# The first expert block of a decoder step: rows by one-hot products, its down product ahead of the second block

## The reference, cut to what matters

```python
def hierarchical_moe(h, w_rg, b_rg, w_re, b_re, w_gate, w_up, w_down):
    t = h.reshape(B * S, D)                       # D = 1024, h = RMSNorm(x) * (1 + scale2) + shift2
    g_logits = (t @ w_rg) + b_rg                  # 4 groups
    g_probs, g_sel = softmax(g_logits), argmax(g_logits)
    e_logits = ((t @ w_re) + b_re).reshape(-1, 4, 8)   # 8 experts in each group, the chosen group's are used
    top_p, top_i = top_k(softmax(e_logits), 2)
    gate = one_hot(g_sel * 8 + top_i) * (g_w * top_p / sum(top_p))
    for g in range(4):
        hid = silu(t @ w_gate) * (t @ w_up)       # per expert 1024 -> 256
        out += (hid * gate) @ w_down              # per expert 256 -> 1024
# x += gate2 * moe(h)
```

## Time and profile before

| | us |
|---|---|
| median of 3 runs (lowest, highest) | 767.51 (767.08, 767.58) |
| the profiled execution, its whole time | 769.74 |
| its span in the profile | 768.0 |
| TensorE busy in the span | 740.7 (96%) |
| VectorE, ScalarE, GpSimd busy | 409.4, 205.9, 166.9 |
| TensorE's share of the chain that ended last | 78% |
| transfers' share of that chain | 7% |

### The profile page before, as it was taken

One profiled execution on the slowest core, in us unless ns is written; L12 is line 12 of the kernel. 1 busy time (PEld: TensorE's weight loads), 2 busy tenths in 40 slices (PEclk: granted clock), 3 DMA queues, 4 the chain that ended last, 5 costly groups with the idle time before them and its releaser, 6 DMA issues.

```text
span 768.0 us, 11157 instructions
## 1 busy us (share of the span) xinstructions
PE 740.7 (96%) x4239; PEld 464.9 (61%) x4239; DVE 409.4 (53%) x955; ACT 205.9 (27%) x419; POOL 166.9 (22%) x188
## 2 busy tenths in 40 slices
PE   7999999999999999997999999999999999999986
PEld 6545465688756657885888544657555555555541
DVE  4124399999999998610254234874432232222235
ACT  4012253306567676002000011222111111111112
POOL 2031021140000000074400002543333333333210
PEclk9999999999999999998999999999999999999999
DMA  8972064123256265453232843359999999999988
GB/s 332 429 252 96 0 218 159 34 91 116 108 212 229 110 242 203 142 181 105 94 101 101 321 190 131 133 183 357 422 422 427 425 424 423 425 425 424 423 336 329
DMA packets 29673, 187.72 MB, mean 244 GB/s; under 512 B 7296, under 2 KB 8384, under 8 KB 18224
## 3 DMA queue, kind: packets, MB, share of 16 engines
q1 hardware_dynamic: 19168, 164.98, 53.8%
q0 software_dynamic: 9536, 19.72, 7.8%
q10 hardware_dynamic: 912, 2.26, 0.8%
HBM read 180.89 MB, written 16.13 MB: 257 GB/s over the span
## 4 chain that ended last, share of the span: by engine, by line
PE 78%; DVE 8%; DMA 7%; issue 3%; ACT 3%; SPq 1%; POOL 0%; DVEq 0%; ACTq 0%; POOLq 0%
PE psum L842 23%; PE psum L1334 13%; PE psum L809 12%; PE psum L1348 7%; DMA ring<-in_experts 5%; PE psum L754 3%; PE psum L1233 3%; PE psum L675 2%; PE psum L1327 2%; DMA ring<-expert_rows 2%; DVE arena L2339 1%; DVE arena L2337 1%; DVE arena L2338 1%; PE psum L658 1%; PE psum L940 1%
## 5 line engine op out<-in xcount | busy, mean ns | idle before, releaser
L842 PE MATMUL psum<-hT,ring 128*128 128x260 f32 x640 | 147.1, 389 | 5.9 <-issue 3.8
L842 PEld LDWEIGHTS psum<-hT,ring 128*128 128x128 f32 x640 | 122.2, 193 | 30.3 <-issue 8.8
L1818 ACT ACTIVATE arena<-psum 128x512 f32<-128x512 f32 (+10 forms) x127 | 68.2, 571 | 228.6 <-PE psum L658 50.9
L809 PE MATMUL psum<-ring,hT 128*128 128x512 f32 (+1 forms) x256 | 93.1, 517 | 0.0
L809 PEld LDWEIGHTS psum<-ring,hT 128*128 128x128 f32 x256 | 47.4, 190 | 41.8 <-issue 32.6
L1334 PE MATMUL psum<-ring,arena 128*64 128x256 f32 x608 | 69.0, 379 | 2.2 <-DMA ring<-in_experts 1.4
L1348 PE MATMUL psum<-arena 128*64 128x512 f32 x280 | 67.8, 605 | 1.4 <-issue 1.4
L1750 POOL DMA_INDIRECT expert_rows<-arena,router x34 | 34.5, 1014 | 139.7 <-DVE arena L2850 123.3
L1334 PEld LDWEIGHTS psum<-ring,arena 128*64 128x64 f32 x608 | 43.8, 137 | 31.3 <-issue 10.1
L2843 DVE COPY arena<-psum 128x128 f32<-128x128 f32 x35 | 10.2, 292 | 95.6 <-PE psum L1341 80.8
L842 PE MATMUL psum<-arena,ring 128*128 128x260 f32 x256 | 58.9, 386 | 0.0
(11 more groups left out here) (402 smaller groups left out, 960.5 us busy)
## 6 DMA issues: line engine op xcount, KB each, us to landing
ring<-in_stream SPq DMA_DIRECT2D x20, 2048.0 KB, 8.9
ring<-in_experts SPq DMA_DIRECT2D x16, 2048.0 KB
arena<-in_experts SPq DMA_DIRECT2D x32, 1024.0 KB
arena<-in_experts SPq DMA_DIRECT2D x11, 2048.0 KB
hT<-in_experts SPq DMA_DIRECT2D x5, 2048.0 KB
ring<-expert_rows SPq DMA_DIRECT2D x8, 512.0 KB, 7.0
ring<-in_stream SPq DMA_DIRECT2D x2, 1280.0 KB, 6.3
arena<-in_x_prompt SPq DMA_DIRECT2D x4, 512.0 KB, 5.9
```

What stands on the lines that cost most here:

```text
L809: mm = pe.matmul(psum[:, b, 0:width], hT[:, k, t * P:(t + 1) * P], w[:, k, :], start=(k == 0), stop=(k == KD - 1))
L842: mm = pe.matmul(psum[:, b0 + s, 0:HALF], w[:, k, f * P:(f + 1) * P], rhs[:, k, s * HALF:(s + 1) * HALF], start=(first and k == 0), stop=( ...
L1818: ins = act.activation(out, in_, func, scale=scale)
```

## The change: what it does

Block 0 belongs to expert 0, which is fixed, so its rows can be found before the tables exist.

- **One-hot rows.** `to_slots` adds for each tile the token's slot with expert 0 (`first_slot`) and a 128x64 table, one where the slot matches, times the token's reciprocal root (`first_hot`). TensorE multiplies it with x2 of the tile (`first_rows`, two 64x512 products a tile, summed over four tiles). The samples come by `first_samples` (eight 128x64 products from normed rows that now lie in partitions 64 to 71, with the shift in others). ScalarE evicts both, TensorE turns the rows, and eight VectorE operations scale them by scale2 and add the samples and the shift into `x_T` for block 0. The fillers idle5, idle6 and idle7 go, and so does the gather of block 0. GpSimd issues one more small load (the shift) before the stage.
- **Samples' norm.** `second_norm_samples` replaces the scaling and the norm of the samples: two operations, both after the samples' reciprocal root.
- **Two loads early.** Loads 4 and 5 go out in two halves each. Load 4 waits for nothing after load 3; load 5 waits for the samples' spread, the last choice and the last norm, no longer for the tables, the first gather and the gate sums.
- **Down product of block 0.** It comes ahead of block 1's gate/up, its eviction too, and the down weights of position 6 are asked for right behind its gate/up weights.
- **Last tile.** `second_scale(4)` is split: one half ahead of the second residual, one behind it.
- gate2's spread is one step on one bank (`adaP`), ahead of the last tile's turning, and the last gate sum comes after block 0's gate/up.

```diff
+            def first_samples(*ks):
+
+                if ks[0] == 0:
+                    pe.wait_ge(*first_hot_ready(1))
+                    pe.wait_ge(t2_ready, 2)
+                    banks.begin(pe, "first_s", 0)
+                for k in ks:
+                    f = 4 * (k % 2) + k // 2
+                    mm = pe.matmul(psum[:, 0, k * SB:(k + 1) * SB], x2[HD:P, NT, f * P:(f + 1) * P], first_hot_s[HD:P],
+                                   start=True, stop=True)
+                if ks[-1] == KD - 1:
+                    banks.filled(mm, "first_s")
+
+            def first_rows(t):
+
+                pe.wait_ge(*first_hot_ready(ROUTE.index((P, t))))
+                if t == 0:
+                    banks.begin(pe, "first", 1)
+                for h in range(2):
+                    mm = pe.matmul(psum[SB * h:SB * h + SB, 1, :], first_hot[t], x2[:, t, 512 * h:512 * h + 512],
+                                   start=(t == 0), stop=(t == NT - 1), tile_position=(0, SB * h))
+                if t == NT - 1:
+                    banks.filled(mm, "first")
...
             gate_sums(2)
+            wide_spread(0)
             x2_transposes(4)
             pick_sums(3)
 
             router_logits(4)
-            wide_spread(10, 0)
-            samples_spread(10, 2, 1)
-            wide_spread(11, 5)
+            samples_spread(10, 2, 5)
+            first_rows(0)
+            first_rows(1)
+            first_samples(0, 1, 2)
             places(4)
             pe.wait_ge(chosen_ready, T5 + 1)
             banks.begin(pe, "counts", 6)
             pe.matmul(psum[0:NE, 6, 0:NE], C("ones")[:, 0:NE], so_far[:, T5 - 1, :], start=True, stop=True)
             banks.filled(pe.matmul(psum[0:NE, 6, NE:NE + 1], so_far[:, T5 - 1, :], C("ones")[:, 0:1], start=True, stop=True),
                          "counts")
-            keep_busy("idle5", 4, 3)
+            first_samples(3, 4, 5, 6, 7)
+            gate_sums(3)
+            first_rows(NT - 2)
+            first_rows(NT - 1)
             pick_sums(4)
-            keep_busy("idle6", 4, 2)
+
+            banks.wait_drained(pe, "first")
+            banks.wait_drained(pe, "first_s")
+            for c in range(4):
+                mm = pe.transpose(psum[:, 0, c * P:(c + 1) * P], y_rows[:, 1, c * P:(c + 1) * P], ident)
+            mm.then_inc(xT_full, 1)
 
             banks.wait_drained(pe, "picks")
             pe.wait_ge(items_ready, 1)
@@ -1327,8 +1379,10 @@
                     mm = pe.transpose(psum[:, p, c * P:(c + 1) * P], x_rows[:, rows, c * P:(c + 1) * P], ident)
                 mm.then_inc(full, 1)
 
-            def gate_up(p, w, full):
+            def gate_up(p, w, full, first=False):
                 for k in range(KD):
+                    if first:
+                        pe.wait_ge(*first_xT(k))
                     for half in range(2):
...
-            gate_sums(3)
-            gate_sums(4)
-            keep_busy("idle7", 6, 16)
-            for name in ("order", "tables", ("adaP", 10), ("adaP", 11), ("adaS", 10)):
-                banks.wait_drained(pe, name)
-            pe.wait_ge(x_got[0], 16)
-            x_transposes(0, 0, xT_full)
-
...
                         over_items()
-                    gate_up(p, w_gu[pos % BUFFERS], gu_full)
-                    if b == 0:
-                        gate_items()
-                        over_code()
-                    elif b == 2:
+                    gate_up(p, w_gu[pos % BUFFERS], gu_full, first=(b == 0))
+                    if b == 2:
                         over_sums()
-                if b >= 1:
+                if b == 0:
+                    gate_sums(4)
+                    for name in ("order", "tables", ("adaS", 10)):
+                        banks.wait_drained(pe, name)
+                    pe.wait_ge(hidden_done, 1)
+                    hidden_transposes(0, hT_full)
+                elif b >= 2:
                     if b >= 3:
                         pe.wait_ge(hT_out, b - 2)
                     pe.wait_ge(hidden_done, b)
                     hidden_transposes(1 - p, hT_full)
                 if b + 1 < N_MAIN:
-                    if b >= 1:
-                        pe.wait_ge(xT_out, b)
+                    if b >= 2:
+                        pe.wait_ge(xT_out, b - 1)
                     rows = (b + 1) % X_BUFFERS
                     pe.wait_ge(*rows_got(b + 1))
                     x_transposes(1 - p, rows, xT_full)
-                if b >= 1:
+                if b == 0:
...
+            def load_by_halves(k):
+                for h in range(2):
+                    cols = slice(GU // 2 * h, GU // 2 * h + GU // 2)
+                    sp.dma_start(w_gu[k].rearrange("p k n -> p (k n)")[:, cols], expert_src(k)[:, cols]).then_inc(gu_got[k], 16)
...
-            sp.wait_ge(t2_stored[0], 16 * 3)
-            load_gate_up(4, 4, gu_got[4])
-            sp.wait_ge(items_ready, 1)
-            sp.wait_ge(exp_ready2, T5)
-            banks.wait_full(sp, ("adaP", 11))
-            sp.wait_ge(x_got[0], 16)
+            load_by_halves(4)
+            banks.wait_full(sp, ("adaS", 10))
+            sp.wait_ge(best_ready, T5)
+            sp.wait_ge(t2_ready, T5)
+            load_by_halves(5)
             banks.wait_drained(sp, "order")
-            banks.wait_full(sp, "gate_sums")
-            load_gate_up(5, 5, gu_got[5])
             def next_down(pos, expert):
...
+                if pos == FIRST:
+                    next_down(pos, expert)
+                elif FIRST + 1 < pos < LAST_POS:
...
+            pool.wait_ge(*shift_scale_in)
+            pool.dma_start(x2[HD:P, NT, :].rearrange("p (c n) -> p c n", c=2),
+                           by_group[MODS.index("shift2"), NS].partition_broadcast(P - HD)).then_inc(late_in, 16)
...
-            for b in range(X_BUFFERS):
+            for b in range(1, X_BUFFERS + 1):
                 gather(b)
...
+            exponents(4)
+            evac("first_s", [(x_T[:, 0], psum[:, 0, :].rearrange("p (k n) -> p k n", k=KD))])
+            evac("first", [(y_rows[:, 1, :], psum[:, 1, :])])
...
+            def second_scale(i, halves=(0, 1)):
+                t = ROUTE[i][1]
                 if i >= 2:
                     dve.wait_ge(t2_stored[i % 2], 16 * (i // 2))
-                lane.mark(dve.tensor_tensor(t2[i % 2][0:n], x2[0:n, t, :], mod2["scale2"][t == NT][0:n], ALU.mult))
+                for c in halves:
+                    cols = slice(512 * c, 512 * c + 512)
+                    dve.wait_ge(x2_ready if c else x2_half, i + 1)
+                    lane.mark(dve.tensor_tensor(t2[i % 2][:, cols], x2[:, t, cols], mod2["scale2"][0][:, cols], ALU.mult))
...
+            def second_norm_samples():
+                dve.wait_ge(rstd2_ready, 2)
+                dve.wait_ge(late_in, 32)
+                lane.then(dve.scalar_tensor_tensor(normed_s, x2[0:NS, NT, :], rstd[0:NS, NT:NT + 1],
+                                                   mod2["scale2"][1][0:NS], ALU.mult, ALU.mult))
+                dve.tensor_tensor(normed_s, normed_s, mod2["shift2"][1][s_rows], ALU.add).then_inc(t2_ready, 1)
...
+                lane.then(dve.scalar_tensor_tensor(junk32[0:n, 0:2], place[0:n, t], 1.0, of_first[0:n, t], ALU.add, ALU.mult,
+                                                   accum_out=first_slot[0:n, t:t + 1]))
+                by_order = lambda a: a.rearrange("p (a m j) -> p a m j", a=2, m=8)
+                if t < NT:
+                    dve.tensor_scalar(by_order(first_hot[t]), slot_order, first_slot[:, t:t + 1], rstd[:, t:t + 1],
+                                      ALU.is_equal, ALU.mult).then_inc(c_silu, 1)
+                else:
+                    lane.then(dve.tensor_scalar(by_order(first_hot_s[s_rows]), slot_order[0:n], first_slot[0:n, t:t + 1],
+                                                None, ALU.is_equal))
+                    dve.tensor_scalar(first_hot_s[s_shift], first_hot_s[s_rows], -1.0, 1.0 / NS, ALU.mult, ALU.add)\
+                       .then_inc(c_silu, 1)
...
+            dve.wait_ge(xT_full, 1)
+            banks.wait_drained(dve, "first_s")
+            for k in range(KD):
+                f = 4 * (k % 2) + k // 2
+                dve.scalar_tensor_tensor(x_T[:, 0, k, :], psum[:, 0, k * SB:(k + 1) * SB], scale_T[:, f:f + 1],
+                                         x_T[:, 0, k, :], ALU.mult, ALU.add).then_inc(x_scaled, 1)
...
+                    if b == 0:
+                        dve.wait_ge(hT_full, 1)
+                        hidden_out(0, hT_out)
```

112 lines of the change are left out of this document (64 added, 48 removed).

## The result

The changed kernel took 770.53 us, median of 20 runs (765.68 to 776.60), beside 767.37 us for 20 runs of the kernel before (764.00 to 770.59). The ratio is 1.0037, 95% interval [1.0021, 1.0054]. I forecast 766.2, which is 0.2% faster; it is 0.37% slower, and outside my range. The profiled execution took 772.47 us (span 770.7, mean granted clock 0.985), against 769.74 (768.0, 0.990) before.

The account below looks back on a forecast made before the run. Expert weight transfers were taken to bound the kernel, TensorE following. Their unbroken run was to end 4.95 - 3.1 - 0.5 = 1.3 us earlier, taking 767.51 to 766.2 us; range 763.5 to 768.9, the forecast's own 765.0 to 767.4.

Parts of the forecast that it names:

- R: Start of the last tile's second residual on VectorE, at 506.76 us before the change; forecast to move by +1.0 us.
- S: Start of the first second-half residual on VectorE, a measuring mark ahead of the change, set after the forecast.
- Routing before the last tile: Added VectorE operations cost 2.6 us, 1.5 covered by its waits for TensorE: R moves +1.0, bounds 0 to +2.6.
- The slower rival: TensorE's clock falls between R + 3 and the first gate/up's end, fillers gone; two falls give 769.4 us; chance 0.14.
- R to the first gate/up: Block 0's gate/up on TensorE starts at R + 15.5 instead of R + 18.7, 2.2 us earlier in time; bounds 2.0 to 4.3.
- First to third gate/up: Gate/up of blocks 1 and 2 start at R + 24.8 and R + 29.9, against R + 25.0 and R + 31.2.
- the rival that gives all back: Block 1's gathered rows land 1.3 us later than assumed, 4.3 us after issue, giving 767.5 us; chance 0.18.
- The loads: The unbroken run of weight loads starts with load 6 instead of load 5 and ends 4.95 - 3.1 - 0.5 = 1.3 us earlier.
- dry queue: Transfer queue runs empty 1.3 us before load 7, against 0.8 before; the difference costs 0.5 us.
- The sum: Transfers decide the end: -1.3 us in all, 767.51 to 766.2 us; bounds of the steps -3.8 to +2.0.
- the signs that I had named against it: First gate/up before 521 or after 525, clock at 0.50 between 508 and 530, or last gate/up waiting for no load.
- More is won: The clock fall in routing at 500 to 502 disappears, R moves -0.5 rather than +1.0, giving 764.4 us; chance 0.18.

Follow-up runs that it names:

- e1_fill: Changed kernel plus eleven filler matmuls in four TensorE waits of the routing stage; 766.36 us, ratio 0.9984 to the kernel before.
- e7: Kernel before the change plus eleven filler matmuls in four TensorE waits of the routing stage; 765.90 us, ratio 0.9992.
- e2_norm: Changed kernel with the samples' norm as before, one operation less behind its wait, no fillers; 769.04 us, ratio 1.0005 to the kernel before.
- e5_late_loads: Changed kernel with the eleven fillers, and loads 4 and 5 asked for late again; 771.68 us, ratio 1.0068 to the kernel before.
- e11: Repeat of the kernel before the change with the same eleven filler matmuls; 766.82 us, ratio 1.0008.
- e4_before_op: Kernel before plus one unused 8 x 1024 VectorE operation between the samples' norm and the first choice; 768.53 us, ratio 1.0019.

## Why the prediction was wrong

| step, us | forecast | changed | e1_fill |
|---|---|---|---|
| R - S (37.44 before) | 38.44 | 41.94 | 37.21 |
| first gate/up - R | 15.5 | 18.16 | 16.55 |
| second gate/up - R | 24.8 | 27.04 | 25.44 |
| third gate/up - R | 29.9 | 32.60 | 30.43 |
| load 6 asked for - R | 19.5 | 22.05 | 20.45 |
| load 6 to last gate/up | 214.9 | 215.26 | 215.22 |
| last gate/up - S (274.15 before) | 272.85 | 279.25 | 272.88 |

**Routing before the last tile.** This is the step that failed. I counted VectorE's operations and put R at +1.0, at most +2.6; it moved by +4.5 in both profiles. The operations were overpriced: at full clock in both, R - S goes from 36.56 (e7) to 37.21 (e1), +0.65. What I left out is that TensorE, in lockstep with VectorE in this stage, gets into a fall of its clock three times as long as the old one: 41.94 - 37.21 = 4.7 us, near half of its 10.2. Together with the second fall it moves the end: 279.25 - 272.88 = 6.4, near half of 13.6. That a fall is what the time goes to is shown, by the fillers and by e2_norm; what sets one off is not, for e2_norm has the same waits and no fall.

**The slower rival.** Its mechanism was right, the clock, its direction too, and its place only in part: I looked for the fall between R + 3 and the first gate/up, where fillers go. One of 3.4 us is there and costs 18.16 - 16.55 = 1.6, the price I gave. The longer one lies ahead of R. I had written against it that after 504 TensorE waited several times without a fall, which says nothing of the stretch before, and gave it 0.14; the earlier trace rows showed a fall in that very stage, and I treated it as a fixed cost that at best goes away. The Trainium skill (TensorE: Matmul & The Clock Gate, "What's actually happening") has activity release a throttle that is the default state; I called that half borne out. That more matmuls in the waits keep the clock up agrees with it, in eight profiles of eight; the long fall itself, 10.2 us in which the records show TensorE busy throughout (10.00 of the 10 us from 498 to 508), it does not explain, and no run here does.

**R to the first gate/up.** 1.05 us too short even at full clock. My lower bound for this step was a slip: one-hot rows that cost twice, 3.8 us more, would have left no gain at all, not 2.0. The samples' eight 64-column products take 0.81 and 1.25 us (514.07 to 514.88 and 515.66 to 516.91 in e1_fill); I had put 0.4 and 0.65. The pick sum started at R + 3.96 (I had 3.8), the one-hot rows took 1.94.

**First to third gate/up.** Right within 0.5: 8.89 and 4.99 us in e1_fill against 9.3 and 5.1. Block 1's gather took 2.74 us from its start (523.78) to the turning of its rows (526.52), where I had 3.0 and the rival that gives all back 4.3; the transfers fell idle as it began (0 GB/s from 524 to 525), so how a load ahead would delay a gather was not tested.

**The loads.** Right: from load 6 to the last gate/up 215.2 against 214.9, the last ones wait for weights, and the tail kept its 24 to 25 us. e5_late_loads showed the term that carries the sum, load 5's 4.95 us less 1.3 for the dry queue, as one difference of 3.62; each of the two alone was not measured.

**The sum.** -1.3 us was forecast and S + 272.88 is 1.27 less than before, since R's overpricing (0.23 below the old one, which holds a fall, instead of 1.0 above) makes up for the 0.95 that load 6 is late and 0.3 behind it. That these cancel to 0.03 is luck. As a forecast of the schedule it held in its size and by that luck; as one of the kernel it did not, for two thirds of the kernel's runs are in the low class of clock. Two of the signs that I had named against it came true, a first gate/up after 525 (526.71) and a clock at 0.50 between 508 and 530 (514.9 to 518.3).

**More is won.** This rival took the fall's end to be worth 1.6 us to the end. In e7 and e11, where it goes without the change, it is worth nothing there. With the change and no fall (e1_fill) R moves by -0.23, not by -0.5.

## What to carry to other kernels

Where two engines work in lockstep, each waiting for the other by under 1 us, price a change of their order by the clock too, and take a fall that the profile already shows there as a warning: here 3.4 us before became 10.2 in both profiles of the changed kernel. It was a matter of odds, not a rule, since one operation more in the old order (e4_before_op) left the fall as it was. Fillers in the waits ahead of a fall are a cheap first experiment, on the changed kernel and on the old one, since a schedule's gain can be hidden behind the clock. And compare positions from a mark ahead of the change: the two pairs of repeats with fillers agree within 0.3 us at the last gate/up, while runs scatter by up to 10 us. But one profile shows the falls of its own run alone, so read the clock of all runs beside it.
